# Head norms of the last attention: squares split into a rounded part and a rest, summed by two rounded products

## The reference, cut to what matters

```python
def rmsnorm(x, g):
    xf = x.astype(jnp.float32)
    y = xf * lax.rsqrt(jnp.mean(xf * xf, axis=-1, keepdims=True) + EPS)
    return (y * g.astype(jnp.float32)).astype(x.dtype)

k = apply_partial_rope(rmsnorm(k.reshape(b_, s_, A_HEADS, A_DH), k_norm_g), cos, sin)
# and for the queries, in moba_mixer, the same with q_norm_g
```

## Time and profile before

| | |
|---|---|
| time, median of 3 runs | 1151.89 us (1151.52 to 1153.32) |
| profiled execution | span 1149.4 us; its time with what surrounds the span isn't on the page, the median lies 2.5 us above the span |
| PE, DVE, ACT, POOL busy in it | 98%, 80%, 60%, 12% |
| granted clock of PE, mean | 0.999 |

### The profile page before, as it was taken

How to read it: one execution, slowest core, us unless ns; L and a number is a source line. 1 busy time by engine, 2 the same in 40 slices (tenths; PEclk the granted TensorE clock), 3 DMA queues, 4 the chain that set the end, 5 groups by cost and what they waited for, 6 DMA issues and landing times.

```text
span 1149.4 us, 23633 instructions
## 1 busy us (share of the span) xinstructions
PE 1131.6 (98%) x9384; PEld 1047.1 (91%) x9384; DVE 914.2 (80%) x1491; ACT 692.6 (60%) x1073; POOL 143.0 (12%) x121
## 2 busy tenths in 40 slices
PE   9999998999999999999999999999999999999998
PEld 8988788978899999889788999998899789999987
DVE  5989764568879999867758899997679968999963
ACT  6787954366656666634557576664355776666642
POOL 2334110000020000002102200000138131000000
PEclk9999999999999999999999999999999999999999
DMA  8743211236555555555432555555554424555552
GB/s 315 238 151 137 96 51 59 93 120 209 187 189 200 184 184 184 179 189 177 163 128 92 185 182 184 184 184 183 184 182 157 157 92 169 184 182 184 184 188 84
DMA packets 55013, 188.96 MB, mean 164 GB/s; under 512 B 6144, under 2 KB 7296, under 8 KB 54784
## 3 DMA queue, kind: packets, MB, share of 16 engines
q1 hardware_dynamic: 53312, 182.48, 45.7%
q10 hardware_dynamic: 1600, 5.05, 1.3%
HBM read 186.46 MB, written 1.05 MB: 163 GB/s over the span
## 4 chain that ended last, share of the span: by engine, by line
PE 80%; DVE 11%; ACT 6%; issue 3%; DMA 1%; SPq 0%; DVEq 0%; ACTq 0%
PE psA L487 71%; PE psB L487 8%; DVE rounded L1890 4%; DVE arena L1890 3%; ACT rounded L1252 2%; ACT arena L1252 2%; DVE arena L1893 2%; ACT L1252 1%; DMA arena<-in_w 1%; DVE arena L2309 0%; DVE rounded L1893 0%; PE psB L797 0%; DVE arena L2510 0%; PE psB L1184 0%; PE psB L780 0%
## 5 line engine op out<-in xcount | busy, mean ns | idle before, releaser
L487 PE MATMUL psA<-rounded,rounded 128*128 128x256 f32 (+1 forms) x7236 | 1004.9, 300 | 6.9 <-DVE rounded L1890 5.6
L487 PEld LDWEIGHTS psA<-rounded,rounded 128*128 128x128 f32 x7236 | 941.6, 191 | 62.6 <-issue 8.0
L1252 ACT ACTIVATE rounded<-arena 128x1024 fp32r<-128x1024 f32 (+2 forms) x508 | 414.6, 857 | 174.0 <-DVE arena L2256 61.9
L1890 DVE TENSOR_TENSOR rounded<-arena,rounded 128x1024 fp32r<-128x1024 f32 (+2 forms) x428 | 468.6, 1121 | 60.1 <-ACT rounded L1252 57.6
L1252 ACT ACTIVATE arena<-arena 128x256 f32<-128x256 f32 (+8 forms) x313 | 162.7, 550 | 169.6 <-DVE arena L2340 104.1
L1893 DVE SCALAR_TENSOR_TENSOR arena<-arena 128x255 f32<-128x255 f32 (+4 forms) x338 | 159.8, 516 | 12.6 <-ACT arena L1252 10.1
L1735 POOL TENSOR_TENSOR arena<-arena 128x512 f32<-128x512 f32 x50 | 67.7, 1368 | 636.5 <-DVE arena L2256 363.5
L487 PE MATMUL psB<-arena 64*64 64x64 f32 (+9 forms) x1664 | 116.4, 264 | 4.2 <-issue 2.3
L487 PEld LDWEIGHTS psB<-arena 64*64 64x64 f32 (+4 forms) x1664 | 83.0, 145 | 27.1 <-issue 17.0
L1890 DVE TENSOR_TENSOR arena<-arena 128x256 f32<-128x256 f32 (+3 forms) x148 | 80.8, 554 | 9.3 <-ACT arena L1252 7.8
L1890 DVE TENSOR_TENSOR arena<-arena,psA 128x256 f32<-128x256 f32 (+1 forms) x101 | 45.3, 449 | 50.4 <-PE psA L487 39.7
(11 more groups left out here) (78 smaller groups left out, 164.9 us busy)
## 6 DMA issues: line engine op xcount, KB each, us to landing
arena<-in_w SPq DMA_DIRECT2D x343, 512.0 KB, 3.5
arena<-in_mem ACTq DMA_DIRECT2D x2, 512.0 KB, 7.8
arena<-in_x ACTq DMA_DIRECT2D x1, 1024.0 KB, 4.8
out<-arena SPq DMA_DIRECT2D x8, 128.0 KB, 2.4
arena<-in_con ACTq DMA_DIRECT2D x1, 992.0 KB, 5.6
arena<-in_con ACTq DMA_DIRECT2D x1, 960.0 KB, 7.1
arena<-in_w SPq DMA_DIRECT2D x2, 256.0 KB, 3.2
arena<-in_x SPq DMA_DIRECT2D x2, 256.0 KB, 4.3
```

Of the source, the lines that this page charges most:

```text
L487: ins_ = nc.tensor.matmul(o, l, r, start=start, stop=stop, skip_group_check=shared)
L1252: return nc.scalar.activation(o, i, f, **kw)
L1890: return V.tensor_tensor(o, a, b, op)
```

## The change

For each pair of heads ACT now makes the square twice: rounded into `asqH` (which lies on the tile `aoH`) and in float32 into `asq`. POOL subtracts the first from the second, with a rounded result, where it made the square before. PE sums both with a rounded matrix of ones (`onesR`), two products into one bank (`reduce_split`), in place of the one in float32. q's squares stand on ACT behind the rotation constants, ahead of the copies of `bk0` to `bk2` and of their splits; each pair waits for DVE's release of its `bq`. k's squares stand behind the exponentials of q: pairs 0 to 2 ahead of the copy of `bk3`, pair 3 behind it. DVE makes two rounded copies of constants near the start. Names of semaphores are shared between stages that follow each other, which adds no instruction; the new helper `square_rest` is not called, and nothing waits for `ones_r`.

```diff
+        SHARED = {"x3": ("x1", 4), "x5": ("x1", 8), "x4": ("x2", 8)}
...
+        asqH = aoH
...
+            def reduce_split(names, lhs, upper_, rest, s, n0=0, per=2):
+
+                for u, name in enumerate(names):
+                    o = open_(name)
+                    ready(pe, s, per * (n0 + u + 1))
+                    mm(o[:, :], fr(lhs), fr(pair_of(upper_, u)), True, False)
+                    close(mm(o[:, :], fr(lhs), fr(pair_of(rest, u)), False, True), name)
...
-            reduce_pairs([f"bqn{u}" for u in range(4)], ones, asq["q"], "a_sq")
+            reduce_split([f"bqn{u}" for u in range(4)], onesR, asqH, asq["q"], "a_sq", 0, 1)
             project(["bk3"], H)
             project_tok(["bv00", "bv01"], H)
-            reduce_pairs([f"bkn{u}" for u in range(4)], ones, asq["k"], "a_sq", 4)
+            reduce_split([f"bkn{u}" for u in range(4)], onesR, asqH, asq["k"], "a_sq", 4, 1)
...
+            def square_upper(s, dst, src):
+
+                A(fr(dst), src, ACT.Square).then_inc(sem(f"{s}_upper"), 1)
...
+            for u in range(4):
+                split_to(SLOT_END[f"bq{u}"] + 2)
+                act.wait_ge(*freed(f"bq{u}"))
+                square_upper("a_sq", asqH[:, pair[u], :], aq[:, pair[u], :])
+                A(asq["q"][:, pair[u], :], aq[:, pair[u], :], ACT.Square).then_inc(sem("a_sq_upper"), 1)
             copies(["bk0", "bk1", "bk2"], [ak[:, c, :] for c in pair[:3]])
             inverse_root([f"bqn{u}" for u in range(4)], asq["q"], P, "a_inv", SLOT_END["bk3"] + 1)
-            copies(["bk3"], [ak[:, pair[3], :]])
+            for u in range(4):
+                if u == 3:
+                    copies(["bk3"], [ak[:, pair[3], :]])
+                act.wait_ge(*freed(f"bk{u}"))
+                square_upper("a_sq", asqH[:, pair[u], :], ak[:, pair[u], :])
+                A(asq["k"][:, pair[u], :], ak[:, pair[u], :], ACT.Square).then_inc(sem("a_sq_upper"), 1)
             split_to(SLOT_END["bk3"] + 7)
...
-                    mul(asq[x][:, s, :], src[:, s, :], src[:, s, :]).then_inc(sem("a_sq"), 1)
+                    ready(pool, "a_sq_upper", 2 * (u + (5 if x == "k" else 1)))
+                    nc.gpsimd.tensor_tensor(fr(asq[x][:, s, :]), asq[x][:, s, :], rd(asqH[:, s, :]), ALU.subtract)\
+                        .then_inc(sem("a_sq"), 1)
                     mul(atm[x][:, s, :], src[:, s, :], bc(cosg[x], 2)).then_inc(sem("a_cos"), 1)
...
+            V.tensor_copy(fr(bonesR), bones).then_inc(sem("ones_r"), 1)
+            V.tensor_copy(fr(onesR), ones).then_inc(sem("ones_r"), 1)
```

More of the change, by code:

```diff
@@ L39 @@
 ORDER = (1, 2, 0)
+SQ_INCS = 7
 DECAY = float(np.exp(-0.5))
@@ L185, in program @@
         sems = {}
+        SHARED = {"x3": ("x1", 4), "x5": ("x1", 8), "x4": ("x2", 8)}
+        for _n, _each in (("xg_f%d", 8), ("xg_f%d_upper", 8), ("sq_f%d", SQ_INCS)):
+            for _f in (1, 2):
+                SHARED[_n % _f] = (_n % 0, _f * _each)
         def sem(name):
+            name = SHARED[name][0] if name in SHARED else name
             if name not in sems:
@@ L241, in program @@
         places = [(4 * i, 4 * i + 4) for i in range(RING + HRING)] + [
-            (62.5, 78.5), (78.5, 104.5), (104.5, 160.5), (160.5, 206)]
+            (62.5, 78.5), (78.5, 104.5), (104.5, 160.5), (160.5, 206), (56.5, 57.5)]
         rounded = [nc.alloc_sbuf_tensor_at(f"rounded{i}", [P, int((b - a) * KB)], F32R,
@@ L256, in program @@
         par = view(57.75, 1, NPAR)
-        assert NCON1 <= 9.75 * KB and NPAR <= 2.75 * KB
+        assert NCON1 <= 8.5 * KB and NPAR <= 2.75 * KB
+        onesR, bonesR = view(56.5, 1, P), view(57, 1, P)
         small = view(60.5, 1, 128)
@@ L406, in both, with pair_of @@
                            ap=[list(a.ap[0]), [abs(a.offset - b.offset), 2]] + [list(y) for y in a.ap[1:]])
+        def pair_of(x, u):
+            return x[u] if isinstance(x, list) else x[:, 2 * u:2 * u + 2, :]
         def memT(k):
@@ L420, in ready @@
         def ready(eng, name, n=1):
-            eng.wait_ge(sem(name), n)
+            eng.wait_ge(sem(name), n + (SHARED[name][1] if name in SHARED else 0))
         def up_units(body, first, last=None):
@@ L624, in sum_squares @@
                 o = open_(name)
-                ready(pe, f"sq_{tag}", 4 if tag in ("x", "m") else 7)
+                ready(pe, f"sq_{tag}", 4 if tag in ("x", "m") else SQ_INCS)
                 for k in range(2):
@@ L1742, in rest_of, with square_rest @@
                         .then_inc(sem(done), 1)
+            def square_rest(s, n, upper_, sq):
+                ready(pool, f"{s}_upper", n + 1)
+                ready(pool, s, 2 * n + 1)
+                nc.gpsimd.tensor_tensor(fr(sq), sq, rd(upper_), ALU.subtract).then_inc(sem(s), 1)
             def square(tag, dst, src, u):
```

## The result

The changed kernel takes 1165.08 us (median of four runs, 1164.22 to 1167.69) against 1151.70 for the kernel before beside it: a ratio of 1.0115 [1.0098, 1.0133], 13.4 us slower. The sum had 10.1, so 3.3 us are missing from it.

A forecast was written before the change was run, and what follows sets the result against it. The prediction took ACT, then DVE, to bound the stage up to the first row maximum, not PE. Term A 4.0 + Term C 3.2 + Term D 2.9 = +10.1 us, giving 1162.0 us, range 1156.5 to 1165.5.

The forecast's parts named there:

- The sum: Added delay up to the first row maximum: +10.1 us, span 1159.5, time 1162.0, bounds 1158.3 to 1164.0.
- What bounds: Between 862 and 918 us ACT, then DVE end last, so PE's saved 3.2 us count 0.
- Term A: ACT's six q squares ahead of bk0's splits stop PE, perhaps halving its clock: 4.0 us, ends 2.3 and 5.0.
- Term C: Six k squares on ACT ahead of the split of bv0's second slot, which DVE awaits: 3.2 us in full.
- Term D: POOL's k operations start late and five meet DVE's: 2.9 us, ends 0.9 (three meet) and 3.9 (six).
- either case fits: At bk0, 4.0 us was taken to fit whether or not PE's clock falls after its stop.
- The delay arrives whole: Behind the first row maximum everything follows from DVE's row maxima, so the delay reaches the end unchanged.
- The constants and the last squares at nothing: Two rounded copies near the start: 0, at most 1 us; k's last squares behind bk3's copy: 0, up to 1.1.
- the rival of two more loads: Squares switch ACT's tables, one load before each group: +2.6 us, 1164.6; chance 0.06.
- POOL not meeting DVE: Rival: POOL's operations stay clear of DVE's, leaving 5.5 to 7.2 us, 1157.4 to 1159.1; chance 0.17.
- Faster: Rival: PE is the bound, idle ACT absorbs the squares, PE's 3.2 us come back whole: 1148.7; chance 0.08.
- No change: Rival: PE stop of 2.3 less 1.6 saved at q, second group hidden: about +0.7 us, 1152.6; chance 0.05.

The follow-up runs named there:

- early_k: Changed kernel, but ACT splits bk0's first slots before q's squares and squares each k pair right behind its copy, into separate tiles: 1.0025 of the kernel before.
- split_first: Changed kernel with one line added, so ACT splits bk0's two slots before q's squares: 1.0076 of the kernel before.
- no_rest_k: Changed kernel without POOL's subtractions for k, so PE sums only the rounded part of k's squares: 1.0070 of the kernel before.
- squares_behind: Changed kernel with all of k's squares moved behind bk3's copy and the two splits after it: 1.0110 of the kernel before.
- q_only: Kernel before with the change on q's side alone; k keeps POOL's square and the float32 product: 1.0045 of the kernel before.
- k_only: Kernel before with the change on k's side alone; q keeps POOL's square and the float32 product: 1.0081 of the kernel before.
- kept_busy_short: Changed kernel plus PE products nobody reads, 22 ahead of bk0 and 6 ahead of the scores of head 2: 1.0110 of the kernel before.
- early_k_busy: early_k plus 18 PE products nobody reads ahead of the scores of head 2: 1.0039 of the kernel before.

## Why the prediction was right or wrong, step by step

**What bounds.** Right, and it decided the sign. ACT and DVE ended last between bk2 and the first row maximum; PE's cheaper products saved what was said (a group of eight takes 2.00 in place of 3.60, so one takes (2.00 - 0.40) / 7 = 0.23) and none of it shows at the end, not even in early_k, with most of A, C and D taken away.

**Term A, 4.0 with ends 2.3 and 5.0.** Measured 4.61. The stop was 2.88, a little over the 2.3 of six squares, since bk0's splits met POOL (two in 4.17, the first of them 0.7 longer than alone); the clock fell; and "either case fits" was right to 0.2 us: with the clock kept full PE waits at bk1 instead. split_first shows that the lead of the splits was the cause.

**Term C, 3.2.** Measured 3.12. Nothing hid the squares, as the 1.02 us of DVE's wait in before had said. The wait grew to 6.35 and not to the 4 that the prediction expected, because DVE, free of POOL ahead of it, came sooner; this changed nothing behind it.

**Term D, 2.9 with ends 0.9 and 3.9.** Measured 4.18, above its range and 1.3 over the sum's: one of the two pieces that make up most of the missing 3.3 (A gives 0.6). "One POOL operation alone takes 1.04" took its price from a row of a square, 861.85 in the earlier trace rows, which reads one tile twice. A subtraction or a cosine product reads two tiles and takes 1.28 to 1.30; the trace of before had that price too, in the row at 886.30 shown above, right behind a square of 1.04. POOL's lead was also a little short, 2.91 (903.02 - 900.11) in place of 3.2. With 1.28 POOL's third operation has 0.82 left when DVE comes (at 1.04 it would have been about done), so six meet instead of five: 6 x 1.02 = 6.1 less 1.9 is 4.2. The price of one meeting (0.97 in the sum, 1.02 measured) was good. no_rest_k and squares_behind confirm the term from both sides, with one and with eight meetings. The Trainium skill ("SBUF — State Buffer", section on the two separate sides) says of the port pair that DVE and POOL share that the one that comes second is blocked for a whole instruction and not slowed. The rows agree with it here: behind the first, whose POOL operation was part over (0.66), each DVE operation that meets in after loses the same 1.08 to 1.10, whether it would take 0.68 or 1.22.

**"The delay arrives whole."** Wrong by 1.40, the other of the two. The reason given (the stretch behind the row maximum is spent in turns between engines) holds at full clock, not at half. PE ended its last values products at 918.50 before and 931.57 after, 13.07 later, where the row maximum is 15.09 later. It is 2.0 us ahead of DVE now, which it can only spend as a stop ahead of head 2, 2.21 in place of 0.20. That stop was followed by half clock in the one part of the stage where PE stands in the chain. With one half alone (q_only, k_only) the stop is short or none and the heads are as before; kept_busy_short has neither the long stop nor the fall, and the 1.4 is gone. PE's saving can be one source of the 2.0, but only k's 1.6 of it: q's goes into the stop ahead of the values' second slot (4.53, against 2.98 in k_only). And it doesn't make the stop by itself, as k_only and kept_busy_short have the same saving of k and a hole of 0.55 to 0.60: where the clock falls further up decides as well. The split between the two stays open.

**The constants and the last squares at nothing.** Nothing is left for them that these runs could show: A, C, D and the heads are 13.31, and the timed difference is 13.38. ACT has 41 table loads in both kernels, so the rival of two more loads had no ground.

**The rivals.** POOL not meeting DVE fell (six meetings). Faster fell for the reason given against it: the chain did not leave DVE. No change needed C hidden, and C stood in full. What I had no rival for was a further fall of the clock, behind a stop late in the stage.

**Luck.** The sum's own bounds end at 1164.0. The 1165.08 lies in the range by the margin that was added for late splits; what came instead was D above its end and the heads.

## What to carry to other kernels

Before work is moved to an engine that idles, look at what stands behind it in that engine's own list, and at how far that list runs ahead of the engine that is full: six cheap squares cost 4.6 us in one place and 0.7 one split further on. Take the price of an operation from a row that reads the same operands, one tile or two, and count on what else an engine meets because its start has moved. An engine that gets ahead of the chain spends its lead as a stop, and a slower clock can follow where the engine is needed next (here 2.21 us, and 1.4 lost).

## What the runs showed of the hardware

- POOL's operation on 128x512 in float32 takes 1.04 us when both inputs are the same tile and 1.28 to 1.30 when they are two (rows 885.30, 886.30 and 900.11).
- DVE and POOL do not always take turns. In after they alternate, one operation each. In early_k one subtraction of POOL's lasted 10.32 us while eleven two-input operations of DVE's ran at their price alone (0.67 and 1.21), back to back, in a window where DVE has no idle time:

```profile
896.55 10.32 POOL L1887 TENSOR_TENSOR rounded<-arena,rounded 128x512 fp32r<-128x512 f32 x1 [1.27 <-ACT arena L1274]
```

```profile
896.00:906.90 10.90, 10.90 (x44) 8.83 (x44) 10.90 (x14) 5.78 (x6) 10.35 (x2) 0.88 0.54 172
```

  What decides between the two is open; no run separates it.
- The length of a stop does not by itself settle whether the clock falls. The stop of the earlier trace rows, 2.19 to 2.20 us in every kernel, at a place that no change touched, was followed by a granted clock of 0.50 in eight of the profiles and not in five, the second profile of before among them (1.00 in 251.60 to 254.80, behind a stop of 2.19). Of the 15 stops of 2.6 us and more in these profiles 13 were followed by a fall, or it began inside them; one (2.68 in squares_behind) lies in a fall that had begun before it, and one (3.68 in early_k_busy) was followed by none.
